# State-space parameters three units earlier, eight identity matmuls, and the second and third weight chunk one x part later

## The chip, the core and the metric

The kernel runs on one core of a Trainium2 chip. The metric is the time of one execution on the device, in microseconds (us). The core has TensorE (PE; the profile shows its weight loads as PEld), VectorE (DVE), ScalarE (ACT), GpSimd (POOL) and SyncE (SP), which issues the DMAs. Each engine runs its own list of instructions in order and waits for the others by semaphores.

## What is computed

Two layers on 512 tokens of width 2048, in float32. The first is a hybrid of a gated convolution and a state-space scan, the second a gating unit beside an attention. The change touches the first:

```
h = rmsnorm(x, norm_g)
proj = jnp.einsum('bld,dn->bln', h, w_in)
v, bg, cg, za, u, zb, ga, gb = jnp.split(proj, SPLITS, axis=-1)
...
lam = lax.complex(a_re, a_im);  dt = jnp.exp(log_dt)[:, None]
lam_bar = jnp.exp(lam * dt)
b_bar = ((lam_bar - 1.0) / lam)[..., None] * b
bu = jnp.einsum('gpc,blgc->blgp', b_bar, ug)
h = scan over time of  h = lam_bar * h + bu
y = jnp.einsum('gcp,blgp->blgc', c, h).real + d_skip * ug
```

## The kernel before

**Units.** All weights pass through the core as chunks of 128 x 1024. SyncE loads a chunk to W (three buffers), ScalarE writes its rounded high part WH (`hi`, L816), VectorE the rest WL (`lo`, L1138), and TensorE multiplies it in 8 blocks of 3 matmuls of 512 columns (L512 to L514: high by high, high by low, low by high). One chunk is one unit, numbered from 0. Units 0 to 15 give u (eight projections of two chunks), units 16 to 143 the part that is called a (four projections for each of 16 channels: a tile of v, cg, bg and za), and so on. Each engine's program has a call `unit()` for every chunk. In unit n ScalarE and VectorE split chunk n + 2, for which they wait until TensorE has ended unit n - 1, and SyncE fetches up to chunk n + 5, for which it waits until VectorE has split the chunk that was in the buffer (chunk n + 2).

**What runs beside the units.** The state-space work has a generator `ssm` on each engine, cut into phases. `ssm_phases(n)` says how many phases must be done after the engine's `unit()` number n: PARAM_PHASES of them are spread evenly over units 4 to 26 (PARAM_UNITS), and the phases of 32 tiles over units 26 to 185. On VectorE `ssm_params` is a chain of 21 steps of small instructions (names SM, V, CB, E, W; the helpers' lines are L1193 to L1201). Its first instruction waits for five loads of parameters (`prm`; are, aim, ldt, cre, cim), which SyncE issues in phase 1 (L349). The later steps fill the tables E and W. After the last one GpSimd may build the tables of a tile (TAB; L1866 to L1869: two times three instructions), and VectorE starts tile 0 with TAB and the two banks that TensorE's `drive` filled (V; L1357).

**The B operand.** For every tile SyncE loads u three times and B once (URAW, BRAW), ScalarE writes the high parts (`stack_high`: USTK, BSTK), GpSimd the low part of u (L1852) and VectorE that of B (`stack_low`, L1329). `drive(j)` (L564) on TensorE waits for both. `drive(0)` stands in TensorE's list ahead of the matmuls of unit 26. SyncE's loads for tiles 2 and 3 wait until the low parts of tiles 0 and 1 are done.

**The norm.** x itself is projected; 1/rms of each token is applied afterwards. ScalarE squares x, VectorE adds the squares up (L1419), TensorE sums them over partitions ahead of unit 5 (L542), VectorE makes the inverse root in six small instructions (`inv_rms`, L1176 to L1187, with a root on ScalarE between), and TensorE spreads it ahead of unit 6 (`spread`, L547), for which it waits (`rms_v`, 6). VectorE's `inv_rms` stands after its unit 5.

**The start.** SyncE loads x in nine parts (X_PARTS: k = 0, 1, and then pairs) with the first chunks between them. ScalarE and VectorE write hH and hL of each k and split chunks 0, 1 and 2 ahead of k = 1, 5 and 11. TensorE runs WARM multiplications of the identity (L608) until the first parts are there.

Of the kernel before, what the change touches and what calls it, by code (L numbers as in the profile page):

```python
# [17 lines left out]
NB = 3  # L18
AHEAD = 2
RING = 3  # L20
WARM = 12
P0 = (0, 512, 896, 1152)
AB = (4, 5, 6, 7)
SEQ_BANKS = (0, 1, 2, 7)
X2_POOL = (3, 7, 11, 14)
U_BANKS = (0, 1, 2, 4, 0, 1, 2, 0)
X_PARTS = [(0, 1), (1, 2)] + [(k, k + 2) for k in range(2, 16, 2)]
PARAM_PHASES = 21
PARAM_UNITS = (4, 26)
SSM_GATES = 13  # L30
A_GATES = 16
# [110 lines left out]
def program(nc, t, out):  # L142
# [11 lines left out]
    def nth(name, i, k=None):  # L154

        return sem[name], SIGNALS[name] * i + (SIGNALS[name] if k is None else k)
# [134 lines left out]
    for p, (stage, _) in enumerate(plan.projections):  # L291
        if stage == "seq":
            bank_free[p] = list(before)
            i = seq_p.index(p)
# [13 lines left out]
    def ssm_phases(n):  # L308
        if n < tiles_from:
            return max(0, (n - PARAM_UNITS[0]) * PARAM_PHASES // (tiles_from - PARAM_UNITS[0]))  # L310
        return PARAM_PHASES + (n - tiles_from + 1) * 130 // (tiles_to - tiles_from + 1)

# [4 lines left out]
    def sp_program(e):  # L317
        at_item, at_unit, loads = [0], [0], [0]

        def fetch():  # L320
            i = at_item[0]
            at_item[0] += 1
            if i >= len(plan.items):
                return
            if i - NW in plan.ada_of:
                e.wait_ge(sem["ada_v"], plan.ada_of[i - NW] + 1)
            elif i >= NW:
                e.wait_ge(*lo_done[plan.unit_of[i - NW]])
            if i == 0:
                e.dma_start(W[:, 0, 512:1024], plan.items[0][:, 512:1024]).then_inc(w_in[0], 16)  # L330
            else:
                e.dma_start(W[:, i % NW, :], plan.items[i]).then_inc(w_in[i % NW], 16)
# [14 lines left out]
        def ssm():  # L347
            for dst, src in ((sm(0), "are"), (sm(1), "aim"), (sm(2), "ldt"), (CR[:, 0], "cre"), (CR[:, 1], "cim")):
                e.dma_start(dst, t[src]).then_inc(sem["prm"], 16)  # L349
            for _ in range(PARAM_PHASES - 6):  # L350
                yield
# [36 lines left out]

        e.dma_start(W[:, 0, 0:512], plan.items[0][:, 0:512]).then_inc(sem["w_first"], 16)
        for i, (k, k_end) in enumerate(X_PARTS):  # L390
            if i in (1, 4, 6):
                fetch()
            e.dma_start(XS[:, k:k_end, :], t["xT"][k:k_end].rearrange("k p s -> p k s")).then_inc(x_in[i], 16)
            if i == 0:
                e.dma_start(PC[:, :], t["cols"]).then_inc(sem["par"], 16)
# [92 lines left out]
    def pe_program(e):  # L488
# [62 lines left out]
        def ssm():  # L551
            for _ in range(PARAM_PHASES - 2):
                yield
# [52 lines left out]
        e.wait_ge(*nth("const", 4))  # L606
        for _ in range(WARM):
            e.matmul(bank[7][:, 0:128], IDT[:, :], IDT[:, :], start=True, stop=True)  # L608
# [198 lines left out]
    def act_program(e):  # L807
        at_unit = [0]

        def hi(n):  # L810
            i = plan.item_of[n]
            e.wait_ge(w_in[i % NW], 16 * (i // NW + 1))
            if n >= NB:
                e.wait_ge(sem["used"], n - NB + 1)
            c = slice(512 if n == 0 else 0, 1024)
            e.activation(WH[:, n % NB, c], W[:, i % NW, c], ACT.Copy).then_inc(sem["hi"], 1)  # L816
# [18 lines left out]
        def ssm():  # L835
            for _ in range(PARAM_PHASES - 4):
                yield
# [30 lines left out]
        e.activation(WH[:, 0, 0:512], W[:, 0, 0:512], ACT.Copy).then_inc(sem["hi_first"], 1)  # L868
        e.wait_ge(sem["par"], 16)
        for k in range(16):  # L870
            if k in (1, 5, 11):
                hi({1: 0, 5: 1, 11: 2}[k])
            i = [k in range(*part) for part in X_PARTS].index(True)
            if k == X_PARTS[i][0]:
                e.wait_ge(x_in[i], 16)
            e.activation(hH[:, k, :], XS[:, k, :], ACT.Identity, scale=col["g1"][:, k:k + 1]).then_inc(sem["xh"], 1)
# [42 lines left out]
        for d, p in enumerate(wa_p):  # L919
# [5 lines left out]
            if 1 <= d <= 8:  # L925
                i = d - 1
# [48 lines left out]
        k = 4  # L975
# [149 lines left out]
    def dve_program(e):  # L1125
# [9 lines left out]
        def lo(n):  # L1135
            e.wait_ge(sem["hi"], n + 1)
            s, c = n % NB, slice(512 if n == 0 else 0, 1024)
            e.tensor_tensor(WL[:, s, c], W[:, plan.item_of[n] % NW, c], WH[:, s, c].bitcast(F32),  # L1138
                            ALU.subtract).then_inc(sem["lo_v"], 1)
# [185 lines left out]
        def stack_low(j):  # L1325
            s = j % 2
            bl = BSTK[64:96, s, :, :]
            e.wait_ge(*nth("ssm_a", j))
            e.tensor_tensor(bl, BRAW[64:96, s, :, :], bl.bitcast(F32), ALU.subtract).then_inc(sem["ssm_lb"], 1)  # L1329

        def ssm():
            phase = 0
            for _ in ssm_params():
                phase += 1
                if phase == PARAM_PHASES - 4:
                    stack_low(0)
                    stack_low(1)
                yield
            assert phase == PARAM_PHASES, phase
            v = [V[:, i, :] for i in range(4)]  # L1340

            def skip_term(ut):
                e.wait_ge(*nth("ssm_out", ut))
                e.wait_ge(*nth("u_rd", ut))
                e.scalar_tensor_tensor(out=U[:, ut, :], in0=U[:, ut, :], scalar=col["dsk"][:, ut:ut + 1],
                                       in1=bank[3][:, :], op0=ALU.mult, op1=ALU.add).then_inc(sem["skip"], 1)

            for j in range(32):
                c, s = TAB[:, j % 2, 0, :], TAB[:, j % 2, 1, :]
                br, bi = bank[4 + 2 * (j % 2)][:, :], bank[5 + 2 * (j % 2)][:, :]  # L1350
                hr, hi_ = HH[j % 4][:, 0, :], HH[j % 4][:, 1, :]
                decay = mag[:, j:j + 1].to_broadcast([128, 512])
                e.wait_ge(*nth("ssm_p", j))
                e.wait_ge(*nth("ssm_bu", j))
                if j > 0:
                    e.wait_ge(*nth("ssm_v", j - 1))
                e.tensor_tensor(v[0], c, br, ALU.mult).then_inc(sem["ssm_v"], 1)  # L1357
                e.tensor_tensor(v[1], s, bi, ALU.mult).then_inc(sem["ssm_v"], 1)
                e.tensor_tensor(v[2], c, bi, ALU.mult).then_inc(sem["ssm_v"], 1)
                e.tensor_tensor(v[3], s, br, ALU.mult).then_inc(sem["ssm_v"], 1)  # L1360
                yield
                if j + 2 < 32:
                    stack_low(j + 2)
                e.wait_ge(*nth("ssm_v", j, 2))
                e.tensor_tensor(v[0], v[0], v[1], ALU.add).then_inc(sem["ssm_v"], 1)
                e.wait_ge(*nth("ssm_v", j, 4))
                e.tensor_tensor(v[2], v[2], v[3], ALU.subtract).then_inc(sem["ssm_v"], 1)
                e.wait_ge(*nth("ssm_v", j, 5))
                e.tensor_tensor_scan(v[1], decay, v[0], 0.0, ALU.mult, ALU.add).then_inc(sem["ssm_v"], 1)
                yield  # L1370
                e.wait_ge(*nth("ssm_v", j, 6))
                e.tensor_tensor_scan(v[3], decay, v[2], 0.0, ALU.mult, ALU.add).then_inc(sem["ssm_v"], 1)
                e.wait_ge(*nth("ssm_v", j, 7))
                e.tensor_tensor(v[0], c, v[1], ALU.mult).then_inc(sem["ssm_v"], 1)
                e.wait_ge(*nth("ssm_v", j, 8))
                e.tensor_tensor(v[2], s, v[3], ALU.mult).then_inc(sem["ssm_v"], 1)
                yield
                if j >= 4:
                    e.wait_ge(*nth("ssm_out", j // 4 - 1))
                e.wait_ge(*nth("ssm_v", j, 10))  # L1380
                e.tensor_tensor(hr, v[0], v[2], ALU.subtract).then_inc(sem["ssm_v"], 1)
                e.wait_ge(*nth("ssm_v", j, 11))
                e.tensor_tensor(v[0], s, v[1], ALU.mult).then_inc(sem["ssm_v"], 1)
                e.tensor_tensor(v[2], c, v[3], ALU.mult).then_inc(sem["ssm_v"], 1)  # L1384
                e.wait_ge(*nth("ssm_v", j, 13))
                e.tensor_tensor(hi_, v[0], v[2], ALU.add).then_inc(sem["ssm_v"], 1)
                if j >= 1 and j % 4 == 0:
                    skip_term(j // 4 - 1)
                yield
            yield  # L1390
            skip_term(7)

        beside, done = ssm(), [0]

        def ssm_until(n):
# [6 lines left out]
                        ALU.subtract).then_inc(sem["lo_first"], 1)  # L1402
        e.wait_ge(sem["par"], 16)
        for k in range(16):
            if k in (1, 5, 11):
                lo({1: 0, 5: 1, 11: 2}[k])
            e.wait_ge(*nth("xh", k))
            e.scalar_tensor_tensor(out=hL[:, k, :], in0=XS[:, k, :], scalar=col["g1"][:, k:k + 1],
                                   in1=hH[:, k, :].bitcast(F32), op0=ALU.mult,
                                   op1=ALU.subtract).then_inc(sem["xl"], 1)  # L1410
# [87 lines left out]
        for d, p in enumerate(wa_p):  # L1498
            unit()
            if 1 <= d <= 8:  # L1500
                i = d - 1
# [119 lines left out]
        k = 4  # L1621
# [327 lines left out]

    counts, final_v, final_p, close_v = {}, {}, {}, {}  # L1950
    dve_program(nc.vector)
    pool_program(nc.gpsimd)
    act_program(nc.scalar)
    pe_program(nc.tensor)
    sp_program(nc.sync)


# [64 lines left out]
```

## Time and profile before

| | us |
|---|---|
| median of 3 runs | 2669.88 |
| lowest, highest | 2667.31, 2670.07 |
| the profiled execution | 2670.03 |
| its span | 2668.8 |
| TensorE busy | 2631.5 (99%) |
| VectorE busy | 1638.4 (61%) |
| ScalarE busy | 845.1 (32%) |
| GpSimd busy | 390.9 (15%) |
| mean granted clock of TensorE | 0.993 |

The sum of busy times is not what sets the end here: TensorE is never idle for long, so the reader looks for the few places where it stands, and asks which engine's list it stood for. The views used are the page, the view of waits (who waited for whom, total, times, longest), the timeline (start, duration, engine, line, operation, count, and in brackets the idle time before it with what ended it), and the view of stretches with the granted clock.

### The profile page before, as it was taken

Reading aid. Unit: us, or ns where it says so; the run is one execution under the profiler, and the core shown is the slowest. Engines: PE = TensorE matmul, PEld = TensorE weight load, DVE = VectorE, ACT = ScalarE, POOL = GpSimd, SP = SyncE. Lnnn points to the kernel's source line nnn. Section 1 sums busy time; section 2 is a strip of 40 time slices with the busy share of each in tenths; the row PEclk is TensorE's granted clock in tenths of the full one; section 3 lists DMA queues with packets and bytes.
Section 4 is the critical chain, followed back from the end, with each engine's and each line's share of the span. In section 5 each row is a group of like instructions: output and inputs, shape, how many; then the busy total and the mean of one; then the engine's idle time right before and its main releaser. Section 6 shows DMA issues by size and latency. Waiting matters only on the chain.

```text
span 2668.8 us, 30016 instructions
## 1 busy us (share of the span) xinstructions
PE 2631.5 (99%) x11928; PEld 2159.8 (81%) x11928; DVE 1638.4 (61%) x2187; ACT 845.1 (32%) x1139; POOL 390.9 (15%) x295
## 2 busy tenths in 40 slices
PE   9989999999999999999999999999999999999997
PEld 7878888888888888888888888877888888888786
DVE  6678888787887765445444775556465563234434
ACT  5122222222222222222322332332565563233321
POOL 0034343433443421000000000010000000000001
PEclk9999999999999999999999999989999999999999
DMA  5233333333333333667555675623222222322333
GB/s 184 96 112 112 105 114 99 121 110 104 116 103 125 128 121 120 215 202 245 186 193 192 207 240 181 197 95 129 95 80 73 86 80 87 111 95 87 115 122 111
DMA packets 119867, 353.07 MB, mean 132 GB/s; under 512 B 15408, under 2 KB 22832, under 8 KB 119728
## 3 DMA queue, kind: packets, MB, share of 16 engines
q1 hardware_dynamic: 119728, 351.16, 39.7%
q8 instruction: 94, 1.54, 0.2%
q14 instruction: 45, 0.37, 0.0%
HBM read 321.68 MB, written 23.07 MB: 129 GB/s over the span
## 4 chain that ended last, share of the span: by engine, by line
PE 96%; DVE 2%; issue 1%; POOL 0%; ACT 0%; DMA 0%; SPq 0%; DVEq 0%; POOLq 0%; ACTq 0%
PE bank L512 29%; PE bank L513 28%; PE bank L514 28%; PE bank L678 2%; PE bank L680 2%; PE bank L679 2%; PE bank L721 1%; PE bank L711 1%; PE bank L576 1%; PE bank L564 1%; DVE X L1814 0%; PE bank L704 0%; PE bank L702 0%; PE bank L502 0%; DMA W<-in_w 0%
## 5 line engine op out<-in xcount | busy, mean ns | idle before, releaser
L1138 DVE TENSOR_TENSOR WL<-W,WH 128x1024 fp32r<-128x1024 f32 (+1 forms) x456 | 592.2, 1301 | 528.3 <-ACT WH L816 527.0
L816 ACT ACTIVATE WH<-W 128x1024 fp32r<-128x1024 f32 (+1 forms) x456 | 480.6, 1056 | 1008.6 <-PE bank L514 768.8
L512 PE MATMUL bank<-hH,WH 128*128 128x512 f32 x1792 | 700.3, 391 | 10.7 <-DVE WL L1138 6.8
L513 PE MATMUL bank<-hL,WH 128*128 128x512 f32 x1792 | 699.1, 390 | 0.0
L514 PE MATMUL bank<-hH,WL 128*128 128x512 f32 x1792 | 698.8, 390 | 0.0
L512 PEld LDWEIGHTS bank<-hH,WH 128*128 128x128 f32 x1792 | 337.1, 188 | 89.9 <-DVE WL L1138 7.2
L514 PEld LDWEIGHTS bank<-hH,WL 128*128 128x128 f32 x1792 | 337.1, 188 | 70.6
L513 PEld LDWEIGHTS bank<-hL,WH 128*128 128x128 f32 x1792 | 337.2, 188 | 70.2
L512 PE MATMUL bank<-h2H,WH 128*128 128x512 f32 x640 | 252.6, 395 | 0.1
L514 PE MATMUL bank<-h2H,WL 128*128 128x512 f32 x640 | 249.4, 390 | 0.0
L513 PE MATMUL bank<-h2L,WH 128*128 128x512 f32 x640 | 249.1, 389 | 0.0
L512 PEld LDWEIGHTS bank<-h2H,WH 128*128 128x128 f32 x640 | 120.2, 188 | 25.9 <-issue 1.9
L514 PEld LDWEIGHTS bank<-h2H,WL 128*128 128x128 f32 x640 | 120.1, 188 | 25.7
L513 PEld LDWEIGHTS bank<-h2L,WH 128*128 128x128 f32 x640 | 120.3, 188 | 24.1
L1866 POOL TENSOR_TENSOR TAB<-E,W 128x512 f32<-128x512 f32 x64 | 83.0, 1297 | 307.6 <-DVE V L1384 293.6
L1921 POOL TENSOR_SCALAR YK<-X,PC,ST 128x512 f32<-128x512 f32 x16 | 12.4, 774 | 746.4 <-DVE X L1549 746.4
L1153 DVE SCALAR_TENSOR_TENSOR ACC<-W,SC,ACC 128x1024 f32<-128x1024 f32 x90 | 115.0, 1278 | 0.0
L512 PE MATMUL bank<-yH,WH 128*128 128x512 f32 (+1 forms) x272 | 102.8, 378 | 2.0 <-DVE yL L1770 2.0
L1869 POOL TENSOR_TENSOR TAB<-TAB,T 128x512 f32<-128x512 f32 x64 | 103.6, 1618 | 5.0
L678 PE MATMUL bank<-WH,h2H 128*128 128x512 f32 x256 | 100.6, 393 | 3.4 <-issue 2.6
L513 PE MATMUL bank<-yL,WH 128*128 128x512 f32 (+1 forms) x272 | 102.4, 377 | 0.0
L514 PE MATMUL bank<-yH,WL 128*128 128x512 f32 (+1 forms) x272 | 102.4, 377 | 0.0
(260 smaller groups left out, 3604.5 us busy)
## 6 DMA issues: line engine op xcount, KB each, us to landing
W<-in_w SPq DMA_DIRECT2D x335, 512.0 KB, 3.7
W<-in_ada SPq DMA_DIRECT2D x96, 512.0 KB, 4.4
W<-in_wa SPq DMA_DIRECT2D x32, 512.0 KB, 3.9
W<-in_wo SPq DMA_DIRECT2D x32, 512.0 KB, 3.9
W<-in_wvv SPq DMA_DIRECT2D x32, 512.0 KB, 3.7
W<-in_wb SPq DMA_DIRECT2D x16, 512.0 KB, 3.7
URAW<-U SPq DMA_DIRECT2D x96, 64.0 KB, 3.1
scr_am<-SO SPq DMA_DIRECT2D x16, 256.0 KB, 2.0
```

The costliest lines, as they stand in the source:

```text
L512: e.matmul(o, wh, xh, start=first, stop=False)
L513: e.matmul(o, wh, xl, start=False, stop=False)
L514: return e.matmul(o, wl, xh, start=False, stop=last)
L564: mm = e.matmul(bank[b + z][:, :], BSTK[:, s, z, :], USTK[:, s, :], start=True, stop=True)
L678: e.matmul(o, h2H[:, k, q4[q]], wh, start=k == 0, stop=False)
L679: e.matmul(o, h2H[:, k, q4[q]], wl, start=False, stop=False)
L680: mm = e.matmul(o, h2L[:, k, q4[q]], wh, start=False, stop=k == 15)
L816: e.activation(WH[:, n % NB, c], W[:, i % NW, c], ACT.Copy).then_inc(sem["hi"], 1)
L1138: e.tensor_tensor(WL[:, s, c], W[:, plan.item_of[n] % NW, c], WH[:, s, c].bitcast(F32), ALU.subtract).then_inc(sem["lo_v"], 1)
L1153: e.scalar_tensor_tensor(out=ACC[:, :], in0=w, scalar=c, in1=ACC[:, :], op0=ALU.mult, op1=ALU.add).then_inc(sem["ada_v"], 1)
L1866: e.tensor_tensor(o, er_, wi if part else wr, ALU.mult).then_inc(sem["ssm_p"], 1)
L1869: e.tensor_tensor(o, o, y, ALU.add if part else ALU.subtract).then_inc(sem["ssm_p"], 1)
```

## The change

WARM goes from 12 to 8. PARAM_PHASES goes from 21 to 24 while the parameters keep their 21 steps (PARAM_STEPS), so that 24 phases are spread over the same units 4 to 26 and the last three are empty on VectorE, but for `stack_low(0)` and `stack_low(1)`, which move from behind step 17 to the second of the empty phases. On the other engines the phases before the tiles are counted from PARAM_PHASES: SyncE's loads for the first tiles, ScalarE's `stack_high` and GpSimd's low parts follow by three phases. The tiles keep their units. On SyncE chunk 1 is fetched before x part 5 in place of 4, and chunk 2 before part 7 in place of 6; ScalarE and VectorE split chunk 1 ahead of k = 8 in place of 5, and chunk 2 ahead of k = 13 in place of 11.

```diff
-WARM = 12
+WARM = 8
...
-PARAM_PHASES = 21
+PARAM_STEPS = 21
+PARAM_PHASES = 24
...
-            if i in (1, 4, 6):
+            if i in (1, 5, 7):
                 fetch()
...
-            if k in (1, 5, 11):
-                hi({1: 0, 5: 1, 11: 2}[k])
+            if k in (1, 8, 13):
+                hi({1: 0, 8: 1, 13: 2}[k])
...
             for _ in ssm_params():
                 phase += 1
-                if phase == PARAM_PHASES - 4:
+                yield
+            assert phase == PARAM_STEPS, phase
+            for i in range(PARAM_PHASES - PARAM_STEPS):
+                if i == 1:
                     stack_low(0)
                     stack_low(1)
                 yield
-            assert phase == PARAM_PHASES, phase
...
-            if k in (1, 5, 11):
-                lo({1: 0, 5: 1, 11: 2}[k])
+            if k in (1, 8, 13):
+                lo({1: 0, 8: 1, 13: 2}[k])
```

Line numbers in the changed kernel are one to three higher than before, so that L547 is L548 there and L564 is L565. The first place is VectorE's list around its units 4 to 6. WL is the low part of a chunk, ST the inverse root (`inv_rms`), SM the parameters; the brackets name the semaphores waited for. Before:

```order
L1138 TENSOR_TENSOR WL<-W,WH 128x1024 [waits s_hi] x3
L1176 TENSOR_SCALAR ST<-bank 128x4 [waits s_sums]
L1183 RECIPROCAL ST<-ST 128x4 [waits s_rms_a,s_rms_v]
L1184 TENSOR_TENSOR ST<-ST 128x4 [waits s_rms_v]
L1185 TENSOR_TENSOR ST<-ST 128x4 [waits s_rms_v]
L1186 TENSOR_SCALAR ST<-ST 128x4 [waits s_rms_v]
L1187 TENSOR_TENSOR ST<-ST 128x4 [waits s_rms_v]
L1138 TENSOR_TENSOR WL<-W,WH 128x1024 [waits s_hi,s_rms_v]
L1195 TENSOR_SCALAR SM<-SM 128x32 [waits s_prm]
```

The same stretch of VectorE's list in the changed kernel:

```order
L1139 TENSOR_TENSOR WL<-W,WH 128x1024 [waits s_hi] x3
L1196 TENSOR_SCALAR SM<-SM 128x32 [waits s_prm]
L1196 TENSOR_SCALAR SM<-SM 128x32 [waits s_prm_v]
L1194 TENSOR_SCALAR SM<-SM 128x32 [waits s_prm_v]
L1202 SCALAR_TENSOR_TENSOR SM<-SM 128x32 [waits s_prm_v] x2
L1177 TENSOR_SCALAR ST<-bank 128x4 [waits s_sums,s_prm_v]
L1184 RECIPROCAL ST<-ST 128x4 [waits s_rms_a,s_rms_v]
```

The first parameter step, which waits for the loads (`s_prm`), stood behind the inverse root and the next WL, and now stands ahead of the root.

The second place is VectorE's list in units 25 to 27. V<-TAB is the first instruction of tile 0, BSTK the low parts of B. Before, BSTK stood behind step 17, in unit 22, and the last parameter step (SM) directly ahead of the WL of unit 27:

```order
L1198 TENSOR_TENSOR SM<-SM 128x32 [waits s_prm_v] x4
L1193 TENSOR_SCALAR SM<-SM 128x32 [waits s_prm_v]
L1329 TENSOR_TENSOR BSTK<-BRAW,BSTK 32x256 [waits s_ssm_a,s_prm_v]
L1329 TENSOR_TENSOR BSTK<-BRAW,BSTK 32x256 [waits s_ssm_a]
L1138 TENSOR_TENSOR WL<-W,WH 128x1024 [waits s_hi]
```

```order
L1198 TENSOR_TENSOR W_89<-V 128x32x8 [waits s_prm_v]
L1198 TENSOR_TENSOR SM<-SM 128x32 [waits s_prm_v] x4
L1193 TENSOR_SCALAR SM<-SM 128x32 [waits s_prm_v]
L1138 TENSOR_TENSOR WL<-W,WH 128x1024 [waits s_hi,s_prm_v]
L1357 TENSOR_TENSOR V<-TAB,bank 128x512 [waits s_ssm_bu,s_ssm_p]
```

In the changed kernel VectorE's list reads there:

```order
L1199 TENSOR_TENSOR W_89<-V 128x32x8 [waits s_prm_v]
L1199 TENSOR_TENSOR SM<-SM 128x32 [waits s_prm_v] x4
L1194 TENSOR_SCALAR SM<-SM 128x32 [waits s_prm_v]
L1139 TENSOR_TENSOR WL<-W,WH 128x1024 [waits s_hi,s_prm_v]
L1139 TENSOR_TENSOR WL<-W,WH 128x1024 [waits s_hi]
L1330 TENSOR_TENSOR BSTK<-BRAW,BSTK 32x256 [waits s_ssm_a] x2
L1139 TENSOR_TENSOR WL<-W,WH 128x1024 [waits s_hi]
L1360 TENSOR_TENSOR V<-TAB,bank 128x512 [waits s_ssm_bu,s_ssm_p]
```

The parameters now end in unit 24, three low parts of chunks stand between them and tile 0, and BSTK stands behind the second of these, that of chunk 28.

## Rows read from the trace of the kernel before

**Rows 1.** The page, its head and TensorE's line: busy us, share, instructions.

```profile
span 2668.8 us, 30016 instructions
...
PE 2631.5 (99%) x11928; PEld 2159.8 (81%) x11928; DVE 1638.4 (61%) x2187; ACT 845.1 (32%) x1139; POOL 390.9 (15%) x295
```

**Rows 2.** Waits of TensorE: us in total, times, longest us.

```profile
PE bank L512 <- DVE WL L1138: 6.8, 1, 6.8
PE bank L512 <- DVE hL L1408: 3.9, 3, 1.8
```

**Rows 3.** Timeline of VectorE: start, us, instruction, idle before and releaser in brackets.

```profile
113.86 1.23 DVE L1138 TENSOR_TENSOR WL<-W,WH 128x1024 fp32r<-128x1024 f32 x1 [2.50 <-ACT WH L816]
...
166.22 0.18 DVE L1193 TENSOR_SCALAR SM<-SM 128x32 f32<-128x32 f32 x1
...
174.50 0.69 DVE L1357 TENSOR_TENSOR V<-TAB,bank 128x512 f32<-128x512 f32 x1 [6.83 <-POOL TAB L1869]
```

**Rows 4.** Timeline of GpSimd, first and last of six table instructions of tile 0.

```profile
166.48 2.09 POOL L1866 TENSOR_TENSOR TAB<-E,W 128x512 f32<-128x512 f32 x1 [13.74 <-DVE SM L1193]
...
173.16 1.30 POOL L1869 TENSOR_TENSOR TAB<-TAB,T 128x512 f32<-128x512 f32 x1
```

**Rows 5.** Timeline of TensorE around its long wait.

```profile
178.09 0.39 PE L514 MATMUL bank<-hH,WL 128*128 128x512 f32 x1
185.24 0.80 PE L512 MATMUL bank<-hH,WH 128*128 128x512 f32 x1 [6.75 <-DVE WL L1138]
...
191.37 0.40 PE L514 MATMUL bank<-hH,WL 128*128 128x512 f32 x1
```

**Rows 6.** Stretch 186 to 188 us: length, busy us by engine, granted clock, DMA.

```profile
186.00:188.00 2.00, 2.00 (x7) 1.52 (x6) 2.00 (x3) 0.00 (x0) 0.00 (x0) 0.50 0.77 256
```

**Rows 7.** Timeline of TensorE, half-rate matmuls after a stand of 2.6 us.

```profile
1781.93 0.59 PE L680 MATMUL bank<-WH,h2L 128*128 128x512 f32 x1
...
1785.31 0.43 PE L679 MATMUL bank<-WL,h2H 128*128 128x512 f32 x1
```

**Rows 8.** Timelines of VectorE, TensorE (the spread) and SyncE around units 5 to 7.

```profile
38.07 3.69 DVE L1138 TENSOR_TENSOR WL<-W,WH 128x1024 fp32r<-128x1024 f32 x3
41.67 0.15 DVE L1176 TENSOR_SCALAR ST<-bank 128x4 f32<-128x4 f32 x1
...
43.04 0.16 DVE L1187 TENSOR_TENSOR ST<-ST 128x4 f32<-128x4 f32 x1
47.23 1.22 DVE L1138 TENSOR_TENSOR WL<-W,WH 128x1024 fp32r<-128x1024 f32 x1 [4.03 <-ACT WH L816]
54.81 0.40 DVE L1195 TENSOR_SCALAR SM<-SM 128x32 f32<-128x32 f32 x2 [6.36 <-DMA CR<-in_cim]
...
55.46 0.42 DVE L1201 SCALAR_TENSOR_TENSOR SM<-SM 128x32 f32<-128x32 f32 x2
...
45.81 1.05 PE L547 MATMUL bank<-IDT,ST 128*128 128x128 f32 x8
...
48.85 0.43 SPq L349 DMA_DIRECT2D SM<-in_are  x1
```

**Rows 9.** Timelines at unit 26 (`drive(0)`, high part) and of VectorE's BSTK.

```profile
145.10 0.75 DVE L1329 TENSOR_TENSOR BSTK<-BRAW,BSTK 32x256 fp32r<-32x256 f32 x2
...
155.53 0.63 PE L564 MATMUL bank<-USTK,BSTK 96*128 96x512 f32 x2
...
156.23 1.05 ACT L816 ACTIVATE WH<-W 128x1024 fp32r<-128x1024 f32 x1
```

**Rows 10.** Timelines of VectorE and GpSimd where a low part meets a table.

```profile
203.52 2.07 DVE L1138 TENSOR_TENSOR WL<-W,WH 128x1024 fp32r<-128x1024 f32 x1
...
204.58 2.16 POOL L1869 TENSOR_TENSOR TAB<-TAB,T 128x512 f32<-128x512 f32 x1
```

**Rows 11.** Timelines of TensorE (identity matmuls) and its weight loads (before unit 5).

```profile
1.96 5.35 PE L608 MATMUL bank<-IDT 128*128 128x128 f32 x24 [1.96 <-POOL CAU L1905]
...
39.34 0.97 PEld L542 LDWEIGHTS bank<-ONE,SO 128*128 128x128 f32 x8 [0.42 <-DVE WL L1138]
```

## The prediction

> **What bounds the kernel now.** I read the page first: TensorE is busy for 2631.5 of 2668.8 us [rows 1], so the time is its stream of matmuls plus the few places where it stands. A weight chunk ("unit") is 24 matmuls of 512 columns, 0.227 us from start to start, 5.44 us in all. The view of waits then says which stand is long: one wait of 6.8 us for the low part of a weight chunk, WL, which VectorE makes [rows 2]. It lies in the stretch in which the change works, so I followed it back. VectorE stood 6.83 us before the first state-space tile, until GpSimd had built the tables of that tile [rows 3]. GpSimd began them at 166.48, right behind the last parameter instruction (166.22 + 0.18), and ended them at 174.46, 8.0 us later [rows 3, 4]. The low part of chunk 30 is queued on VectorE behind that tile, so TensorE had nothing from 178.3 to 185.24 [rows 5]. Its clock was granted at half (1.2 GHz) behind that [rows 6], and the 14 steps between the matmuls at 185.24 and 191.37 took 6.13 us in place of 3.17 [rows 5]. The place costs (185.24 - 178.09 - 0.23) + 2.96 = 6.9 + 3.0 = 9.9 us. That is the most that the change can win here.
>
> **Part 1, the wait that goes.** The parameters' 21 steps are spread over units 5 to 24 in place of 6 to 26. Before, the last step ended at 166.40, which is 10.9 us after TensorE began unit 26 (155.53 [rows 9]). In unit 24 the same step ends about 10.9 us after the start of that unit, or just as unit 26 begins. The tables (8.0 us) are then there at about 163.5 on the old time axis, and VectorE asks for them in unit 27, after a low part that can end at 164 at the earliest. Should 1 us of the wait stay, it is covered: a low part can be ready 2.3 us after the start of the unit two ahead of its own, and is wanted 10.9 us after it. I book **-9.9 us**. VectorE now has two steps in unit 15; before, the same two steps were behind it, with time to spare, at 113.86, where it stood 2.50 us [rows 3].
>
> **Part 2, a wait that comes at unit 6.** This stands in the order and not in the words of the change. The first parameter step moves from unit 6 to unit 5 on VectorE. It waits for five loads of parameters, and SyncE issues those only after a weight load that needs the low part of the same VectorE unit. Before, that low part ended at 48.45 (47.23 + 1.22), SyncE issued the five loads from 48.85 on, and the step began at 54.81, 6.36 us after the low part [rows 8]. TensorE didn't notice, since nothing that it needed soon stood behind. Now the step stands ahead of the six small instructions that make 1/rms of the tokens (41.67 to 43.20), and TensorE wants their result for the spread matmuls at 45.81, before unit 6 [rows 8]. New times: the third of three low parts ends at 41.76 (38.07 + 3.69); + 6.36 = 48.12; the step takes 55.88 - 54.81 = 1.07, so 49.2; the rms chain 1.53, so 50.7; a semaphore later TensorE goes on at 50.8. It stands for 50.8 - 45.8 = **5.0 us**. Behind VectorE's wait also stand ScalarE's root, and with it the high and low parts of chunk 8, which are wanted only 10 us later, and the copies of u, which wait for the spread anyway. Bounds: 4.5, if the loads land sooner, and 5.7, if the weight loads that the three low parts set free one after the other hold them back. I take 5.0, from the row itself.
>
> The clock: a stand of this kind was followed by a half-rate stretch in both rows at hand. After 6.9 us without a matmul it cost 3.0 us [rows 5]; after one of 2.6 us it cost 1785.31 - 1781.93 - 8 x 0.227 = 1.6 us [rows 7]. I take the middle, **2.3 us**, with both as ends.
>
> **Part 3, a wait that comes at unit 26.** The low parts of B for tiles 0 and 1 (stack_low) move on VectorE from unit 22 to unit 26, behind the low part of chunk 28. TensorE's first drive matmul stands ahead of unit 26 and waits for the first of them; before, it ran without a wait at 155.53 [rows 9]. Chunk 28 can be split only when TensorE has ended unit 25. So the chain is: high part on ScalarE 156.23 to 157.28 [rows 9], low part 1.2 us, stack_low 0.4 us (half of 0.75 [rows 9]). With nothing else that is 158.8, a stand of 3.3 us. But GpSimd now builds tables in just these microseconds, and next to a table instruction a low part took 2.07 us in place of 1.23 [rows 8, 10]; the low part of chunk 27 goes before it and is slowed too. I add 0.6 for VectorE coming late from there and 0.5 for the second low part: **4.4 us**, with 3.3 as the lower end and 6.0 as the upper (both low parts and stack_low slowed in full, parameters 0.7 us late). Clock again **2.3 us**, from 0 to 3.0: no row has a stand of just this length.
>
> The Trainium skill, page "SBUF — State Buffer", section "Who interferes with whom", says that a VectorE instruction with two SBUF inputs and a GpSimd instruction that reads SBUF exclude each other for a whole instruction. The low part is of that kind, and by that rule it could wait for a whole table instruction of 1.3 us, against the 0.84 us that [rows 8, 10] show; the stand of part 3 would come to 5.3 us by it, an estimate.
>
> **Part 4, the start.** The second and third chunk come one x part later on SyncE, and are split behind k = 7 and k = 12. Unit 1 can begin about 1 us sooner, as k = 5 to 7 no longer stand behind the low part of chunk 1 (1.2 us). But before unit 5 TensorE stood 0.42 us for a low part [rows 11], which hangs on VectorE's chain of squares and not on the start. A win at the start is worth 0.1 us. The four identity matmuls less take 4/12 of 5.35 us [rows 11] = 1.8 us, which TensorE spends standing for x. Their 24 records took 0.22 us each, the same form in the spread 1.05 / 8 = 0.13 [rows 8, 11]: they ran slowly, and the real ones behind them fast. If the shorter run leaves the clock low for the 24 matmuls of unit 0, that is 24 x 0.2 = 4.9 us, of which the three waits for hL take up 3.9 [rows 2]. Booked: 0, from -0.1 to +1.0.
>
> The Trainium skill, page "TensorE: Matmul & The Clock Gate", section "Part 1: The HAM clock gate", says that "the default state is throttled, and activity releases the throttle". By it the shorter warm-up speaks against the change, and the sum would be 1.0 us higher, an estimate.
>
> **At nothing.** SyncE's loads for tiles 2 and 3 now wait for the new stack_low, at some 4.4 us into unit 26, with chunk 30 behind them and behind eight issues of some 0.5 us. Chunk 30 lands some 4 us after its issue, near 7 us into unit 27, and is wanted at unit 28: cover of 3.6 us and the stand itself; past that every microsecond would be TensorE's. GpSimd's low parts of tiles 0 and 1 move to unit 24 and end well before unit 26.
>
> **Sum.** -9.9 + 5.0 + 2.3 + 4.4 + 2.3 + 0 = **+4.1 us** against the profiled run of 2670.03 us (its span is 2668.8): 2674.1. The median is 2669.88, 0.15 us from it, so I forecast 2674.
>
> **Rivals.**
> (a) The forecast, both new waits: 2669.5 to 2678.5. Low end -9.9 + 4.5 + 1.6 + 3.3 + 0 = -0.5.
> (b) Only the wait at unit 26 comes: -9.9 + 4.4 + 2.3, so 2666.8. For it: the loads are small. Against: SyncE issues them behind the same event as before, and that took 6.36 us.
> (c) The change does what its words say and no more: 2670.0 - 9.9 = 2660. Both chains above must be wrong for it.
> (d) Slower: at unit 26 GpSimd's table work blocks the low parts of chunks 27 and 28 and stack_low one after the other: 6.0 + 3.0 there, 5.0 to 5.7 and 3.0 at unit 6, -9.9, and 0.5 to 1.0 from a low clock at the start: +7.6 to +8.8, so 2678. It decides from the point where VectorE ends chunk 27 later than 1.7 us into unit 26, since from there on the stand grows one for one.
> (e) The change doesn't take the table wait away, as the denser steps crowd VectorE and the last one ends in unit 26 after all. Half of the 9.9 stays: 2679.
>
> **Chances.** (a) 0.60, (b) 0.12, (c) 0.06, (d) 0.18, (e) 0.04. A measurement of this kernel tells about 0.2%, 5.3 us, from no change: the bounds are 2664.5 and 2675.2. Faster: (c) and a little of (b), 0.08. Slower: (d), (e) and the quarter of (a) above 2675.2, 0.36. Same: 0.56. The range that holds 8 in 10 leaves out (c), the lower half of (b) and the top of (d): 2666.5 to 2679.
>
> **What would show it.** In the profile after: a wait of TensorE at the spread (L548) of about 5 us near 46, released by VectorE's ST; VectorE standing 6 us for the CR load near 42; a wait of 3.3 to 6 us at the first drive matmul (L565), released by BSTK; no wait of V for TAB; granted clock 0.50 behind either wait, and none near 190. The forecast is wrong if the loads land by 45, or if TensorE runs past 158 without a stand.

## The result, and the profile after

| | us |
|---|---|
| changed kernel, median of 8 runs | 2676.20 (2675.56 to 2676.82) |
| kernel before, median of 8 runs beside them | 2667.73 (2666.93 to 2670.07) |
| ratio | 1.003, 95% interval 1.0019 to 1.0041 |
| span of the profiled execution, before and after | 2668.8 and 2674.3 |

The change makes the kernel 0.3% slower, 8.5 us by the medians. The forecast was 2674 with a range to 2679, and the case was its likeliest one, with both new waits. The view of TensorE's waits (us in total, times, longest) in the changed kernel shows them at the top, and the wait for WL of [rows 2] is gone:

```profile
PE bank L548 <- DVE ST L1188: 6.7, 2, 4.8
PE bank L565 <- DVE BSTK L1330: 6.2, 1, 6.2
PE bank L513 <- DVE hL L1411: 3.0, 2, 2.1
```

L548 is the spread and L565 the drive matmul. (The other 1.9 us of L548 lie at the very end, and stand in both kernels.) The first new wait in the timelines of VectorE, SyncE and TensorE of the changed kernel; these rows answer to [rows 8]:

```profile
40.61 1.23 DVE L1139 TENSOR_TENSOR WL<-W,WH 128x1024 fp32r<-128x1024 f32 x1 [0.20 <-ACT WH L817]
48.06 0.40 DVE L1196 TENSOR_SCALAR SM<-SM 128x32 f32<-128x32 f32 x2 [6.22 <-DMA CR<-in_cim]
...
50.47 0.16 DVE L1188 TENSOR_TENSOR ST<-ST 128x4 f32<-128x4 f32 x1
...
42.23 0.43 SPq L350 DMA_DIRECT2D SM<-in_are  x1
...
50.77 2.05 PE L548 MATMUL bank<-IDT,ST 128*128 128x128 f32 x8 [4.78 <-DVE ST L1188]
52.48 0.77 PE L513 MATMUL bank<-hH,WH 128*128 128x512 f32 x1
```

The reader sees the chain of the prediction: SyncE issues the loads behind the last low part, VectorE stands 6.22 us for them (6.36 in [rows 8]), and the inverse root ends at 50.63 where it ended at 43.20. TensorE had ended unit 5 at 45.84 and goes on at 50.77, 4.9 us later. The spread takes 1.71 us to the next matmul in place of 0.81. Then the second wait, in the timelines of VectorE, GpSimd, ScalarE and TensorE; these rows answer to [rows 3, 4, 9]:

```profile
157.90 2.31 DVE L1139 TENSOR_TENSOR WL<-W,WH 128x1024 fp32r<-128x1024 f32 x1
160.13 1.97 DVE L1199 TENSOR_TENSOR V<-W,SM 128x256 f32<-128x256 f32 x2
...
164.87 0.18 DVE L1194 TENSOR_SCALAR SM<-SM 128x32 f32<-128x32 f32 x1
165.09 3.21 DVE L1139 TENSOR_TENSOR WL<-W,WH 128x1024 fp32r<-128x1024 f32 x2
168.33 2.56 DVE L1330 TENSOR_TENSOR BSTK<-BRAW,BSTK 32x256 fp32r<-32x256 f32 x2
...
157.42 3.93 POOL L1855 TENSOR_TENSOR USTK<-URAW,USTK 32x512 fp32r<-32x512 f32 x2 [0.17 <-ACT USTK L845]
165.13 2.09 POOL L1869 TENSOR_TENSOR TAB<-E,W 128x512 f32<-128x512 f32 x1 [3.78 <-DVE SM L1194]
...
164.05 1.05 ACT L817 ACTIVATE WH<-W 128x1024 fp32r<-128x1024 f32 x1
...
163.13 0.39 PE L515 MATMUL bank<-hH,WL 128*128 128x512 f32 x1
169.74 1.19 PE L565 MATMUL bank<-USTK,BSTK 96*128 96x512 f32 x2 [6.22 <-DVE BSTK L1330]
```

TensorE ended unit 25 at 163.36 and stood until 169.74, 6.4 us. The last parameter step ended at 165.05, the two low parts behind it (chunks 27 and 28) took 3.21 us, and the first of the two instructions on BSTK, asked for by itself, 1.15 us. The high part of chunk 28 on ScalarE was done at 165.10 and held up nobody: VectorE took it up at 166.23. VectorE no longer waits for TAB at all: tile 0 starts behind a low part that itself waited for TensorE.

The granted clock (stretches of the changed kernel: length, busy us of PE, PEld, DVE, ACT and POOL with counts, clock, DMA) is at half behind both stands, and is full where [rows 6] show half:

```profile
50.00:56.00 6.00, 5.22 (x16) 4.52 (x17) 4.88 (x15) 2.60 (x4) 0.00 (x0) 0.50 0.28 87
170.00:172.00 2.00, 2.00 (x5) 1.53 (x5) 0.89 (x1) 0.00 (x0) 1.92 (x3) 0.50 0.27 66
...
184.00:190.00 6.00, 6.00 (x28) 4.95 (x27) 5.83 (x9) 1.06 (x1) 0.29 (x1) 1.00 0.16 42
```

Behind the first stand it cost 0.9 us in the spread and 2.1 us in the ten steps between the matmuls at 52.48 and 56.82; behind the second, 0.5 us in the drive and 1.0 us up to 172.84. The account between the two profiled executions is -9.9 + 4.9 + 3.0 + 6.4 + 1.5 = +5.9 us (each stand with the half rate behind it), and the spans differ by 5.5.

### The profile page after: what moved, and what is told of

It is laid out like the page before. It is cut to its first block, busy times and chain, and to the rows that moved or that the text cites. A ratio compares the mean times of both kernels' runs of the same rounds, so it can differ in the third digit from the quotient of the medians.

```text
span 2674.3 us, 29999 instructions
## 1 busy us (share of the span) xinstructions
PE 2633.2 (98%) x11920; PEld 2161.6 (81%) x11920; DVE 1638.2 (61%) x2187; ACT 844.1 (32%) x1139; POOL 391.9 (15%) x295
## 4 chain that ended last, share of the span: by engine, by line
PE 96%; DVE 2%; ACT 0%; DMA 0%; issue 0%; SPq 0%; POOL 0%; DVEq 0%; ACTq 0%
PE bank L513 29%; PE bank L514 28%; PE bank L515 28%; PE bank L679 2%; PE bank L680 2%; PE bank L681 2%; PE bank L722 1%; PE bank L712 1%; PE bank L565 1%; PE bank L577 1%; DVE WL L1139 0%; DVE X L1817 0%; PE bank L705 0%; PE bank L703 0%; PE bank L503 0%; DVE V L1199 0%
```

## The experiments

The theory to be tested: the loss is made of two waits, each of a known place in VectorE's list, and the gain of 9.9 us is there beside them. The main rival is that TensorE would have stood at those places for something else, or that GpSimd's tables are the real bound. The ratios below are each to the kernel before in the same job, which ran at a median of 2668.96 in the first four and 2668.68 in the other four. The changed kernel itself ran only in the job of the result, where the kernel before was at 2667.73, so a difference to its 2676.20 can be off by about 1 us.

**The inverse root first.** The changed kernel, but VectorE makes the inverse root ahead of the first parameter step again.

```diff
-            ssm_until(unit())
+            n = unit()
             if m == 2:
                 inv_rms(0, 3, 0, 0)
-            else:
+            ssm_until(n)
+            if m > 2:
                 keep_u(m)
```

> The changed kernel with one thing put back: on VectorE the inverse root (inv_rms) stands ahead of the first parameter step again, in unit 5. Theory (the wait for the loads, put ahead of the inverse root, holds TensorE at the spread): the stand of 4.9 us at the spread and the half rate behind it (3.0 us) go, so 7.9 us less than the changed kernel: 2676.2 - 7.9 = 2668, level with the kernel before (2667.7). The stand at the first drive matmul stays near 6.4 us. Rival (TensorE would have stood for something else there, the copies of u or the low part of chunk 8): a stand of 3 us or more stays between 45 and 60 us, and the time falls by less than 4.

Measured: 2668.52, ratio 1.000 (0.9991 to 1.0009). Timeline of VectorE and TensorE in this kernel:

```profile
41.69 0.15 DVE L1177 TENSOR_SCALAR ST<-bank 128x4 f32<-128x4 f32 x1
...
49.54 0.40 DVE L1196 TENSOR_SCALAR SM<-SM 128x32 f32<-128x32 f32 x2 [6.31 <-DMA CR<-in_cim]
...
45.71 0.39 PE L515 MATMUL bank<-hH,WL 128*128 128x512 f32 x1
45.94 1.05 PE L548 MATMUL bank<-IDT,ST 128*128 128x128 f32 x8
```

VectorE still stands 6.3 us for the loads, but behind the root, and nobody notices; the spread follows the matmul before it at once. The stand at the drive is as it was, 6.2 us. By the medians 7.7 us of the loss belong to the place of one step.

**The low parts of B earlier.** The changed kernel, but stack_low for tiles 0 and 1 stands ahead of the last parameter step, in unit 24.

```diff
                 phase += 1
                 yield
+                if phase == PARAM_STEPS - 1:
+                    stack_low(0)
+                    stack_low(1)
             assert phase == PARAM_STEPS, phase
             for i in range(PARAM_PHASES - PARAM_STEPS):
-                if i == 1:
-                    stack_low(0)
-                    stack_low(1)
                 yield
```

> The changed kernel with VectorE's two low parts of B (stack_low) moved from unit 26 to unit 24, ahead of the last parameter step. Theory (the first drive matmul waits for stack_low behind the low part of chunk 28): the stand of 6.4 us and the half rate behind it (1.5 us) go, so 2676.2 - 7.9 = 2668; the stand at the spread stays. VectorE will wait some 3 us for TAB in unit 27, hidden. Rival (GpSimd's tables are the bound there): TensorE stands by 3 us or more in units 28 to 31 for WL, and half or more of the 7.9 is given back.

Measured: 2666.75, ratio 0.9993 (0.9984 to 1.0002), 9.5 us under the changed kernel, 1.6 more than expected. The medians of the kernel before move by 1.3 from job to job (2667.7 to 2669.0), and the spans of the two profiled executions differ by 8.0 (2674.3 and 2666.3). The timelines of VectorE and TensorE:

```profile
160.43 1.72 DVE L1330 TENSOR_TENSOR BSTK<-BRAW,BSTK 32x256 fp32r<-32x256 f32 x2
...
175.96 0.69 DVE L1360 TENSOR_TENSOR V<-TAB,bank 128x512 f32<-128x512 f32 x1 [3.33 <-POOL TAB L1872]
...
163.54 0.63 PE L565 MATMUL bank<-USTK,BSTK 96*128 96x512 f32 x2
164.00 0.39 PE L513 MATMUL bank<-hH,WH 128*128 128x512 f32 x1
```

The drive runs without a wait. VectorE waits 3.33 us for TAB, half of what it did before [rows 3], and TensorE doesn't stand for it.

**Both.**

> Both repairs at once: inverse root first in unit 5, stack_low in unit 24. Theory: all three stands are gone, the one that the change took away and the two that it made: 2676.2 - 15.8 = 2660.4, 7 us (0.27%) under the kernel before. No wait of TensorE over 1 us between 20 and 1700 us, and granted clock 1.00 throughout that stretch. Rival: with TensorE not held up, VectorE is late at units 28 to 30 as in the kernel before, and a stand of 2 us or more for WL comes back; then 2663 to 2667.

Measured: 2660.06 (2659.0 to 2661.13), ratio 0.9967 (0.9954 to 0.9979). This kernel is faster than both: by 0.33% than the one before, by 16 us than the changed one. TensorE's stretches in it, from unit 1 to the end of the first layer and around the two places:

```profile
20.00:1750.00 1730.00, 1728.92 (x7726) 1420.15 (x7726) 1191.57 (x1457) 464.53 (x568) 357.78 (x255) 1.00 0.46 149
40.00:50.00 10.00, 10.00 (x50) 8.37 (x49) 3.51 (x13) 3.25 (x5) 0.00 (x0) 1.00 0.64 208
150.00:190.00 40.00, 39.72 (x175) 32.46 (x174) 34.39 (x43) 8.68 (x11) 21.38 (x15) 1.00 0.38 119
```

It stands for 1.1 us in 1730, at full clock, and 0.28 us of that near unit 30, where the rival looked for 2. The rest of the 1.1 us is mostly the 0.8 us ahead of unit 5, for the low part of chunk 5. By the medians the repairs give 7.7 and 9.5, against 16.1 together. Within this one job the low parts of B are worth 8.5 us on top of the first repair (2668.52 to 2660.06) and the place of the root 6.7 on top of the second (2666.75 to 2660.06). A point inside the profiled executions is sharper than the medians: TensorE's sums for the second layer's norm, the first work behind the first layer's last matmul. Timelines of TensorE in the kernel before, the changed one, the two with one repair and the one with both, in this order:

```profile
1767.44 0.35 PE L542 MATMUL bank<-ONE,SO 128*128 128x1 f32 x2 [1.54 <-ACT T L953]
...
1773.23 0.35 PE L543 MATMUL bank<-ONE,SO 128*128 128x1 f32 x2 [1.54 <-ACT T L954]
...
1765.80 0.35 PE L543 MATMUL bank<-ONE,SO 128*128 128x1 f32 x2 [1.54 <-ACT T L954]
...
1766.17 0.35 PE L543 MATMUL bank<-ONE,SO 128*128 128x1 f32 x2 [1.54 <-ACT T L954]
...
1757.55 0.35 PE L543 MATMUL bank<-ONE,SO 128*128 128x1 f32 x2 [1.54 <-ACT T L954]
```

There the change has cost 5.8 us, the repairs give back 7.4 and 7.1, and both together 15.7, of which 0.6 lie ahead of unit 5. They add up. The kernel with both is 9.9 us ahead of the kernel before.

**The start alone.** The kernel before with eight identity matmuls and the two chunks later, nothing else.

> The kernel before with the start of the change alone: eight identity matmuls, second and third chunk one x part later. Theory: TensorE reaches unit 5 early enough either way and waits there for the low part of chunk 5, so 2667.7 within 1 us. Rival (the shorter warm-up leaves the clock low for longer and this reaches the end): 1 to 3 us slower.

Measured: 2668.03, ratio 0.9998 (0.9989 to 1.0007). No difference that the time shows. The wait for WL of 6.7 us is there as in [rows 2]. In the trace the sums ahead of unit 5 start at 38.73 us, 0.6 us sooner than before [rows 11]; in the changed kernel they start at 39.34, as before.

**The parameters alone.** The changed kernel with the old start: WARM 12, chunks 1 and 2 at their old places.

> The changed kernel with the start of the kernel before (twelve identity matmuls, chunks 1 and 2 ahead of x parts 4 and 6): only the parameter part of the change. Theory (the whole difference is the parameter part): 2676 within 1 us, with the stands of 5 us at the spread and 6 us at the first drive matmul. Rival (a part of the loss is the start's): 2674 or less.

Measured: 2675.91, ratio 1.0027 (1.0016 to 1.0038), with the waits of 5.4 and 6.2 us in its view. The two halves agree: all of the difference is the parameter part's.

**The loads early.** The changed kernel with the order of VectorE left alone, but SyncE issues the five parameter loads behind the last x part.

```diff
         def ssm():
-            for dst, src in ((sm(0), "are"), (sm(1), "aim"), (sm(2), "ldt"), (CR[:, 0], "cre"), (CR[:, 1], "cim")):
-                e.dma_start(dst, t[src]).then_inc(sem["prm"], 16)
...
+        for dst, src in ((sm(0), "are"), (sm(1), "aim"), (sm(2), "ldt"), (CR[:, 0], "cre"), (CR[:, 1], "cim")):
+            e.dma_start(dst, t[src]).then_inc(sem["prm"], 16)
         for p in u_p:
```

> The changed kernel with SyncE's five parameter loads issued right behind the last x part, before chunk 3 and the following ones; VectorE's order is left as the change has it. Theory (the price at the spread is the time that the loads take after the low part of unit 5, not the step itself): VectorE's step follows the low parts without a wait, the inverse root is ready at 41.8 + 1.1 + 1.5 = 44.4, before TensorE asks at 45.8, no stand at the spread, 2676.2 - 7.9 = 2668. Rival (the place of the step is enough to hold the root up, or the loads delay chunk 3 and the x parts): a stand of 1 us or more between 20 and 60 us, and less than 6 us gained.

Measured: 2668.94, ratio 1.0001 (0.9992 to 1.001), 7.3 us gained by the medians. VectorE's timeline:

```profile
38.82 3.49 DVE L1139 TENSOR_TENSOR WL<-W,WH 128x1024 fp32r<-128x1024 f32 x3
42.23 0.39 DVE L1196 TENSOR_SCALAR SM<-SM 128x32 f32<-128x32 f32 x2
...
44.63 0.16 DVE L1188 TENSOR_TENSOR ST<-ST 128x4 f32<-128x4 f32 x1
```

The step follows at once, the root is there at 44.8, and the spread no longer waits. So the stand was the time of the loads, and not the step's own 1.1 us. The rival's stand of 1 us is there too: the three low parts begin at 38.82 in place of 38.06, and TensorE stands 1.06 us ahead of unit 5, with half rate behind it. Whether that is the loads going ahead of chunk 3 isn't shown; with the loads at their old place the sums ahead of unit 5 start anywhere from 38.72 to 39.85 in the traces, here at 40.09 (timeline and stretch of TensorE):

```profile
40.09 1.05 PE L543 MATMUL bank<-ONE,SO 128*128 128x1 f32 x8 [1.06 <-DVE WL L1139]
...
48.15 1.05 PE L548 MATMUL bank<-IDT,ST 128*128 128x128 f32 x8
...
42.00:44.00 2.00, 2.00 (x6) 1.57 (x5) 1.49 (x8) 0.20 (x1) 0.00 (x0) 0.50 0.88 262
```

This profiled execution, the slowest of its eleven (2670.73), has gained 5.0 us at the end of the first layer (1768.20 for 1773.23), less than the 7.4 of the first repair.

**The tables later.** The changed kernel with a later wait on GpSimd: in place of the one for the last of VectorE's squares (`xacc`), which stand ahead of unit 5, the tables of tile 0 begin when VectorE's two low parts of B are done.

```diff
             e.wait_ge(sem["prm_v"], counts["param"])
-            e.wait_ge(*nth("xacc", 15))
+            e.wait_ge(*nth("ssm_lb", 1))
             table(0, 0)
```

> The changed kernel with one more wait on GpSimd: the tables of tile 0 begin only when VectorE's two low parts of B are done, so no table instruction runs beside the low parts of chunks 27 and 28 and stack_low. Theory (the stand of 6.4 us at the first drive matmul is a chain of 3.3 us plus VectorE's being late plus some 2 us of GpSimd and VectorE excluding each other): the two low parts take 2.4 us in place of 3.2 and the two stack_low 0.75 in place of 2.56, the first of them ends 1.8 us sooner, and the stand is 4.6 us. VectorE waits for TAB in unit 27, hidden. Rival (GpSimd has no part in it): the stand stays at 6.2 us or more.

Measured: 2675.07, ratio 1.0024 (1.0015 to 1.0033). The timelines of VectorE and TensorE have the stand and its parts:

```profile
163.95 2.36 DVE L1139 TENSOR_TENSOR WL<-W,WH 128x1024 fp32r<-128x1024 f32 x2
166.34 0.75 DVE L1330 TENSOR_TENSOR BSTK<-BRAW,BSTK 32x256 fp32r<-32x256 f32 x2
...
167.01 1.19 PE L565 MATMUL bank<-USTK,BSTK 96*128 96x512 f32 x2 [4.62 <-DVE BSTK L1330]
```

The stand falls from 6.2 to 4.6 us, as expected. The two low parts take 2.36 us in place of 3.21, and the two instructions on BSTK 0.75 in place of 2.56. So 1.6 us of the second stand are GpSimd's tables running beside VectorE. The rest is VectorE's own list, counted from the end of unit 25: the parameters end 1.7 us behind it, as in the changed kernel, then come two low parts of 1.2 us and 0.4 us for BSTK. The time falls by 1.1 us, less than the 1.6 and too little for the medians to separate from nothing. The end of the first layer comes 1.15 us sooner (1772.08 for 1773.23), with 0.2 us more at the first stand.

**No identity matmuls.** The kernel before with WARM = 0.

> The kernel before without any identity matmul. Theory (the start is not on the path, unit 5 waits for the low part of chunk 5 either way): TensorE's first matmuls run at half rate, the gaps for x take up most of it, and the time is 2667.7 to 2669. Rival (the clock stays low long enough to reach unit 5): 2 to 5 us slower.

Measured: 2668.95, ratio 1.000 (0.9991 to 1.0009). Timeline of TensorE:

```profile
8.31 0.77 PE L512 MATMUL bank<-hH,WH 128*128 128x512 f32 x1 [8.31 <-DVE hL L1408]
8.88 0.63 PE L513 MATMUL bank<-hL,WH 128*128 128x512 f32 x1
9.30 0.63 PE L514 MATMUL bank<-hH,WL 128*128 128x512 f32 x1
...
12.87 0.39 PE L513 MATMUL bank<-hL,WH 128*128 128x512 f32 x1
...
39.37 1.05 PE L542 MATMUL bank<-ONE,SO 128*128 128x1 f32 x8
```

The first nine matmuls run at about half rate by their spacing (0.42 to 0.43 us where none waits, 0.23 from 12.87 on; the view of stretches shows a granted clock of 1.00 for both), and the sums ahead of unit 5 start at 39.37, where they started at 39.34 with twelve identity matmuls [rows 11].

## Why the prediction was right

**The wait that goes** (-9.9). It went, and so did the half rate behind it: no wait for WL, and full clock from 174 to 1760. The kernel with both repairs shows the gain, 8.9 us under the kernel beside it by the medians and 9.9 at the end of the first layer, 0.6 of them from ahead of unit 5, and tells that the change's aim was sound.

**The wait at unit 6** (5.0 + 2.3 forecast, 4.9 + 3.0 measured). The size came out of one row, 6.36 us behind a low part, and held to 0.14 us. Two experiments settle the cause from two sides: take the root out from behind the wait, or take the wait away, and 7 to 8 us come back either way by the medians.

**The wait at unit 26** (4.4 + 2.3 forecast, 6.4 + 1.5 measured). The wait, its place and its releaser were right; the term was mis-sized by 2.0 us, and beyond its upper end of 6.0. The chain that I priced went through ScalarE's high part of chunk 28, with 0.6 us for VectorE "coming late". In the trace that high part is ready 1.1 us before VectorE takes it up, and the stand is VectorE's list: 1.7 us until it had ended the parameters, 3.2 us for the low parts of two chunks, of which I had counted one, and 1.15 us for stack_low, where I had put in 0.4. The 1.7 us are read from the trace and no run takes them away: GpSimd's low parts of u, which moved to unit 24 with the change, ran beside the low part of chunk 26 (2.31 us in place of 1.22) and the first instructions of the last step (1.97 us in place of 0.88). "At nothing" was wrong for them. The rule of the Trainium skill (page "SBUF — State Buffer", section "Who interferes with whom") would have given 5.3 us for the stand, an estimate, and that was nearer than the price that I took. The trace agrees with it in kind: the kernel with later tables puts 1.6 us on the two engines running side by side. In size the low part of chunk 28 lost 0.84 us (2.07 in place of 1.23, as in [rows 10]) and not the 1.3 of that estimate; the rest came from places that neither price had.

**The clock**, 2.3 us each from the middle of two rows: 3.0 and 1.5 measured; that the sum came out right was luck.

**The start** (0). Right, and shown three times: the start alone, its reverse, and no identity matmuls at all stay within 1 us. The 0.1 us for a win there was small: two of the traces with the new start reach unit 5 0.6 us sooner. The rule that the clock must be released by activity (the Trainium skill, page "TensorE: Matmul & The Clock Gate", section "Part 1: The HAM clock gate") agrees with the half-rate matmuls of the last kernel; it costs nothing here, because unit 5 waits for VectorE in any case.

**The number.** The account gives +5.9 us and the spans +5.5, against +4.1 forecast; the 1.8 us between account and forecast are the wait at unit 26 with the clock behind it (7.9 for 6.7) and the clock at unit 6 (3.0 for 2.3), less 0.1 for the stand there. The medians differ by more, 8.5 us, twice the forecast. The other 3 us lie in which executions were profiled: 2670.03 of the kernel before is 2.3 us above the median of its eight runs, 2675.56 of the changed one 0.6 below. The forecast was added to that high run; added to 2667.73 the same sum gives 2671.8, 4.4 us short. So part of the closeness to 2676.2 is luck.

Why runs of one kernel differ by 3 us was not tried, but the record shows what goes with it. Of the 56 runs of the kernel before beside the experiments, the 20 with a mean granted clock of 0.992 or 0.993 took 2669.40 us or more, and the 36 at 0.994 took 2669.35 or less (from 2666.44 on). In the mean clock 0.001 is 5.3 us at half rate, or 2.7 us of work, an estimate from the span of 2668.8.

By the bound of 0.2% that stood in the prediction the outcome is "slower", which had 0.36 against 0.56 for "same"; a sum of +5.9 would have been just past that bound of 5.3. Rival (d), which asked for VectorE to end chunk 27 later than 1.7 us into unit 26, had its condition met, and its price for that stand (6.0) was nearer than the forecast's. Its 3.0 for the clock there (1.5 measured) and its loss at the start were not borne out.

## What to carry to other kernels

A step that waits for a DMA can stand for 6 us unseen as long as nothing that the bounding engine needs stands behind it in its list; before moving such a step earlier, look at what it moves past, and whether the load is issued earlier too. When small work is moved to make room for a stage, look for the place where it lands relative to the instruction that starts at the last possible moment, here the low part that must wait for the previous unit: whatever stands behind that and ahead of the bounding engine is paid in full. And where two engines slow each other in the trace, as VectorE and GpSimd do here, put the moved instructions of the one beside the other's before calling a move free.

## What was not expected of the hardware

An instruction on 32 partitions and 256 columns took 1.15 to 1.49 us beside a table instruction of GpSimd, against 0.41 us without (0.75 for two, which overlap a little). Small instructions lose as much to the neighbour as large ones: about 0.9 us each, near the 1.05 to 1.30 us of one table instruction. The low part of 128 x 1024 lost between 0.6 and 1.1 where it lost anything (1.79, 2.07 and 2.31 us in place of 1.23), and the low part of chunk 27, which began 0.04 us ahead of the first table instruction, lost nothing. GpSimd loses as well: its first table instruction took 2.09 us beside VectorE and 1.05 us in the kernel where it started behind VectorE's work. Spans on GpSimd are rough, but the starts of the next instruction say the same, 2.05 and 1.01 us later.

The half rate behind a stand is not in proportion to it: 3.0 us were lost behind a stand of 4.9 us, 1.5 us behind one of 6.4 us in the same execution, and 3.0 us behind one of 6.9 us before. Nor is it the same each time: behind the same wait for WL it was 2.8 us in the profiled execution of the start alone and 2.4 us in that without identity matmuls.
